# Two-block transformer kernel on one core: first block's output projection in three rounded products, feature by feature, with reordered norm, head-sum and feed-forward steps

## What is computed

```python
def readout(o_sum, g, u):
    o = rmsnorm(o_sum, onorm_g).reshape(Bn, Ln, HG_WIDTH).astype(g.dtype) * jax.nn.silu(g)
    return jnp.concatenate([multiscale_pool(u, pool_w, pool_scale), o], axis=-1) @ w_out
...
x = x + g1 * rmsnorm(y_lat, norm_g[l, 1])
f_lat = swiglu(rmsnorm(x, norm_g[l, 2]) * (1.0 + sc2) + sh2, ffn_w_in[l], ffn_w_out[l])
```

## Time and profile before

| what | value |
|---|---|
| time of the runs, us | 2217.25, 2224.48, 2217.38 (median 2217.38) |
| profiled execution's own time, us | 2223.95 |
| its span in the trace, us | 2222.0 |
| mean granted clock of PE | 0.986 of full |
| bytes read from memory | 370.84 MB |

### The profile page before, as it was taken

One profiled execution on the slowest core, in us unless ns is written; L12 is line 12 of the kernel. 1 busy time (PEld: TensorE's weight loads), 2 busy tenths in 40 slices (PEclk: granted clock), 3 DMA queues, 4 the chain that ended last, 5 costly groups with the idle time before them and its releaser, 6 DMA issues. The chain is left out here.

```text
span 2222.0 us, 32315 instructions
## 1 busy us (share of the span) xinstructions
PE 2151.3 (97%) x13514; PEld 1851.3 (83%) x13514; DVE 1401.9 (63%) x1602; ACT 986.8 (44%) x1114; POOL 173.4 (8%) x94
## 2 busy tenths in 40 slices
PE   6999999999999999999999999999999999999999
PEld 4887788888888857888888898888988897878888
DVE  4367845666766456656665678656665687566665
ACT  3312333444544234444444555445444565254444
POOL 0065600000000000000100011000100012001000
PEclk8999999999999999999999999999999998999999
DMA  8227913455455412355555533555455442124552
GB/s 334 106 100 295 412 74 131 165 191 192 160 189 189 169 72 76 138 192 189 200 189 189 189 133 142 189 189 189 167 191 190 170 166 100 36 91 163 191 192 79
DMA packets 52609, 373.28 MB, mean 168 GB/s; under 512 B 5792, under 2 KB 6816, under 8 KB 7968
## 3 DMA queue, kind: packets, MB, share of 16 engines
q1 hardware_dynamic: 51632, 367.71, 44.9%
q0 software_dynamic: 880, 4.19, 0.5%
HBM read 370.84 MB, written 1.05 MB: 167 GB/s over the span
## 5 line engine op out<-in xcount | busy, mean ns | idle before, releaser
L500 DVE TENSOR_TENSOR ring_r<-ring,AR_r 128x2048 fp32r<-128x2048 f32 x286 | 655.3, 2298 | 267.3 <-ACT AR_r L494 267.1
L494 ACT ACTIVATE AR_r<-ring 128x2048 fp32r<-128x2048 f32 x286 | 545.0, 1911 | 326.2 <-PE PS L397 195.0
L376 PE MATMUL PS<-AR_r 128*128 128x512 f32 x2240 | 533.2, 390 | 0.0
L376 PEld LDWEIGHTS PS<-AR_r 128*128 128x128 f32 x2240 | 415.6, 188 | 83.1
L380 PEld LDWEIGHTS PS<-AR_r,ring_r 128*128 128x128 f32 x2240 | 287.2, 191 | 10.9
L380 PE MATMUL PS<-AR_r,ring_r 128*128 128x256 f32 x2240 | 290.6, 283 | 0.0
L541 ACT ACTIVATE AR<-PS 128x512 f32<-128x512 f32 x140 | 83.7, 598 | 418.6 <-PE PS L380 418.6
L395 PE MATMUL PS<-AR_r 128*128 128x512 f32 x616 | 241.4, 392 | 0.0
L396 PE MATMUL PS<-ring_r,AR_r 128*128 128x512 f32 x616 | 241.1, 391 | 0.0
L397 PE MATMUL PS<-AR_r 128*128 128x512 f32 x616 | 240.4, 390 | 0.0
L397 PEld LDWEIGHTS PS<-AR_r 128*128 128x128 f32 x616 | 116.0, 188 | 24.7
(11 more groups left out here) (394 smaller groups left out, 2927.2 us busy)
## 6 DMA issues: line engine op xcount, KB each, us to landing
ring<-stream SPq DMA_DIRECT2D x346, 1024.0 KB, 4.8
X<-xt SPq DMA_DIRECT2D x1, 2048.0 KB, 9.0
AR<-bias POOLq DMA_DIRECT2D x1, 1536.0 KB, 6.5
AR<-pt POOLq DMA_DIRECT2D x2, 512.0 KB, 4.5
out<-X SPq DMA_DIRECT2D x4, 256.0 KB, 2.1
AR<-invc SPq DMA_DIRECT2D x1, 512.0 KB, 15.3
X<-negl POOLq DMA_DIRECT2D x1, 512.0 KB, 6.3
H<-wax POOLq DMA_DIRECT2D x1, 512.0 KB, 7.2
```

The source lines that it names most:

```text
L376: pe.matmul(PS[:, (6, 4)[half] + j, :], block(w_hi_of(tag, i + half), j, k), X_PARTS[:, k, :], start=(k == 0), stop=False, skip_group_chec ...
L494: act.activation(w_hi_of(tag, i), ring[:, n % SLOTS, :], ACT.Identity).then_inc(split_hi, 1)
L500: dve.tensor_tensor(RING_R[:, n % SLOTS, :], ring[:, n % SLOTS, :], w_hi_of(tag, i), ALU.subtract).then_inc(split_lo, 1)
```

## The change

1. `mix0_out` becomes a split product, by chunks of 256 input features (the host lays the weights out that way): for each chunk 24 products of 128 x 512 (2 token tiles, 2 halves of the output, 2 feature tiles, 3 terms), four chunks of lat, then chunk 0 of ctx, the turn, chunks 1 and 2 of ctx, the norm's sums, chunk 3 of ctx.
2. ACT and DVE get the four weight splits, and the rounding and the rest of the eight input tiles.
3. Order of the norm's steps: all multiplications before the scalings; the additions to X before the splits; in two places the first half of the tokens is scaled before the last statistics.
4. `pe_turn_tokens` after the attention layer, and `pe_turn_both`, wait for each half of the tokens by itself.
5. The low-weights phase at the entry of a feed-forward goes chunk by chunk.
6. `mix3`: half of chunk 13 between the two groups of head sums, the other half between the spreads; the sums wait for the logarithms only; the split of chunk 15 comes before the head norms on ACT and DVE.

```diff
-SPLIT_OUTS = ('mix1_out', 'mix2_out', 'mix3_out')
+SPLIT_OUTS = ('mix0_out', 'mix1_out', 'mix2_out', 'mix3_out')
...
             for i in chunks:
                 pe.wait_ge(split_lo, SPLIT_BASE[tag] + i + 1)
-            for k in range(DT):
-                products(k, True, X_HI)
+                for k in range(DT):
+                    products(k, True, X_HI, of=(i,))
...
+            for q in range(GROUPS):
+                dve.tensor_tensor(SQ[:, pair(q), cols], src[:, pair(q)], r, ALU.mult).then_inc(S["scaled"], S.mark("scaled", (tag, q)))
             for q in range(GROUPS + 1):
                 if q < GROUPS:
-                    dve.tensor_tensor(SQ[:, pair(q), cols], src[:, pair(q)], r, ALU.mult).then_inc(S["scaled"], S.mark("scaled", (tag, q)))
...
+                for k in (*range(4, DT), *range(4)) if apart and t == 0 else range(DT):
+                    if apart and k == 0:
+                        pe.wait_ge(S["normed"], S.at("normed", (tag, t)))
+                    if apart and k == 4:
+                        pe.wait_ge(S["token_high"], S.at("token_high", (tag, t)))
...
+            stats(1, 0)
+            if first_early:
+                scale(0)
+            stats(1, 1)
+            gather(1)
...
+            if nxt:
+                dve_split_chunk(dve, nxt, 1)
+            dve.wait_ge(order.sem, order.n)
             dve.wait_ge(S["residual"], S.at("residual", (tag, GROUPS - 1)))
+            if nxt:
+                dve_split_input(dve, nxt, X[:, :, c])
...
+            def out_chunk(i, key):
+
+                if key == lat:
+                    pe.wait_ge(split_lo, SPLIT_BASE["mix0_out"] + i + 1)
+                    pe.wait_ge(S["mixer_low"], S.at("mixer_low", ("mix0", i)))
+                for t in range(2):
+                    for h in range(2):
+                        first = T + t * P if key == lat else t * P
+                        if i == 0 and key == lat:
+                            pe.wait_ge(S["mixer_output"], S.at("mixer_output", ("mix0 taken", 2 * t + h)))
+                        for f in range(2):
+                            k, ws = 2 * i + f, slice(f * D + h * 512, f * D + (h + 1) * 512)
+                            w_hi, w_lo = w_hi_of("mix0_out", i)[:, ws], RING_R[:, (START["mix0_out"] + i) % SLOTS, ws]
+                            for n, (x, w) in enumerate(((CAT0_HI(k), w_hi), (CAT0_HI(k), w_lo), (CAT0_LO[:, k, :], w_hi))):
+                                ins = pe.matmul(PS[:, (LOW if key == lat else HIGH)[2 * t + h], :], x[:, first:first + P], w, start=(i + f + n == 0),
+                                                stop=(i == 3 and f == 1 and n == 2), skip_group_check=True)
...
+            for i in range(4):
+                out_chunk(i, lat)
+            pe.wait_ge(S["o_rinv"], S.at("o_rinv", HEADS - 1))
+            out_chunk(0, ctx)
             pe_turn_tokens(pe, lat, TOK1[0], LOW)
-            pe_tokens(pe, "mix0_out", ctx, CAT0, 0, 0, 1, 5, False)
+            out_chunk(1, ctx)
+            out_chunk(2, ctx)
             pe_norm(pe, ("ffn0_pre", 0), LAT, 0)
-            for h in range(2):
-                pe_tokens(pe, "mix0_out", ctx, CAT0, 0, 1, h, 6 + h, True)
+            out_chunk(3, ctx)
...
+            for i in range(2):
+                dve_split_chunk(dve, "mix0_out", i)
+            dve.wait_ge(S["mixed"], S.at("mixed", HEADS - 1))
+            for q in range(2):
+                dve.wait_ge(S["x_hi"], S.at("x_hi", ("mix0_out", q)))
+                dve.tensor_tensor(CAT0_LO[:, pair(q), :], CAT0[:, pair(q), :], POOL_HI[:, pair(q), :], ALU.subtract).then_inc(
+                    S["mixer_low"], S.mark("mixer_low", ("mix0", q)))
...
             z_chunk(12)
             head_sums((4, 5, 6, 7))
+            z_half(13, 0)
             head_sums((0, 1, 2, 3))
-            for h in range(4):
+            for h in range(2):
                 spread(h)
+            z_half(13, 1)
             for h in range(0, 2):
                 head_products(h)
-            z_chunk(13)
+                spread(h + 2)
...
-            for i in range(2):
-                dve_split_chunk(dve, "ffn2", i)
-            dve_rms_tokens(dve, order, "ffn1_lat", 0, LOW, TOK1[0], need_tokens(dve, "ffn1_lat", "ffn1_lat", FFN_LAST))
+            dve_split_chunk(dve, "ffn2", 0)
+            dve_rms_tokens(dve, order, "ffn1_lat", 0, LOW, TOK1[0], need_tokens(dve, "ffn1_lat", "ffn1_lat", FFN_LAST), first_early=True)
...
-    parts["mix0_out"] = chunks_in(g["ab_w_out"][0])
+    parts["mix0_out"] = chunks_out(g["ab_w_out"][0])
```

More of the change, by code:

```diff
@@ L293, in pe_chunks_as_features_come, with products @@
             tiles = [(i, j, bank) for i, bank in zip(chunks, banks) for j in range(2)]
-            def products(k, low_weights, x, first=False, last=False):
-                for i, j, bank in tiles:
+            def products(k, low_weights, x, first=False, last=False, of=tuple(chunks)):
+                for i, j, bank in (tile for tile in tiles if tile[0] in of):
                     w = slice(k * 256 + j * P, k * 256 + (j + 1) * P)
@@ L704, in dve_add_turned @@
+            if first_early:
+                scale(0)
+            stats(1, 1)
+            gather(1)
+            if not first_early:
+                scale(0)
+            scale(1)
         def dve_add_turned(dve, order, tag, banks, g, s, nxt=None):
             c = STREAM[s]
[L707 to L719, removed]
+            for q in range(GROUPS):
+                dve.wait_ge(S["turned_back"], S.at("turned_back", (tag, q)))
+                for k in (2 * q, 2 * q + 1):
+                    ins = dve.scalar_tensor_tensor(out=X[:, k, c], in0=PS[:, banks[q], (k % 2) * T:(k % 2 + 1) * T], scalar=mod_of(g, k, s),
+                                                   in1=X[:, k, c], op0=ALU.mult, op1=ALU.add)
+                    if k % 2 == 0:
+                        ins.then_inc(order.sem, order.step())
+                ins.then_inc(S["residual"], S.mark("residual", (tag, q)))
@@ L884, in pe_mix0 @@
-            pe_tokens(pe, "mix0_out", ctx, CAT0, 0, 0, 0, 4, False)
+            def out_chunk(i, key):
[13 more added lines that the diff above has]
+                                                stop=(i == 3 and f == 1 and n == 2), skip_group_check=True)
+                        if i == 3 and (key == lat or (t, h) != (1, 1)):
+                            ins.then_inc(S["tokens_done"], S.mark("tokens_done", (key, t, h)))
+                if key == ctx:
+                    ins.then_inc(multiplied, 1)
@@ L955, in act_mix0 @@
                 act.activation(SQ[:, 4 + h, :], SQ[:, 4 + h, :], ACT.Exp, scale=-0.5).then_inc(S["o_rinv"], S.mark("o_rinv", h))
+            act_split_chunk(act, "mix0_out", 2, free=START["mix0_out"])
+            for h in range(HEADS):
+                act.wait_ge(S["mixer_output"], S.at("mixer_output", (0, h)))
+                act.activation(SQ_R[:, h, :], GS[:, h, :], ACT.Identity).then_inc(S["x_hi"], S.mark("x_hi", ("mix0_out", 2 + h)))
+            act_split_chunk(act, "mix0_out", 3, free=START["mix0_out"])
         def dve_mix0(dve, order):
@@ L1250, in pe_mix1 @@
                 ins.then_inc(multiplied, 1)
-            pe_turn_tokens(pe, "mix1_post", TOK1[0], HIGH)
+            pe_turn_tokens(pe, "mix1_post", TOK1[0], HIGH, apart=True)
             pe_norm(pe, "ffn1_pre", LAT, 0)
@@ L2031, in spread @@
                 if h < 4:
[L2032 removed]
+                    pe.wait_ge(S["head_rinv"], S.at("head_rinv", ("log", h)))
                 else:
```

93 lines of the change are left out of this document (57 added, 36 removed).

## The result

| | runs | median, us | lowest to highest |
|---|---|---|---|
| before | 4 | 2219.95 | 2217.25 to 2224.48 |
| changed | 4 | 2203.82 | 2202.34 to 2205.73 |

The ratio is 0.9926, with an interval of 0.991 to 0.9941: 16.1 us less where 18.9 were forecast. The time of 2203.82 us lies inside the stated range, 5.3 us above the forecast of 2198.5; 2.6 us of that is because the kernel before, with a fourth run, has a median of 2219.95 instead of 2217.38. The profiled execution of the changed kernel took 2202.34 us, its span is 2200.5 us and its granted clock 0.990.

A forecast was written before the change was run, and what follows sets the result against it. PE, busy 97% of the span, was taken to bound the kernel. Terms -6.4 - 3.8 - 1.2 - 7.5 = -18.9 us, off the median of 2217.38, gave 2198.5 us; range 2189 to 2208.

The forecast's parts named there:

- Part 4: `mix3`: half chunks remove the wait between head sums and bring head 4's products sooner; -7.5 us, between -4 and -9.
- A: Rival: `mix0`'s gain is lost in DVE's list, the wait before the feed-forward growing to 12 us; 2205 us, chance 0.13.
- Rival B: `mix3` is bound by DVE and ACT, so half chunks only move PE's wait; 4 us there, 2202 us, chance 0.15.
- Rival D: POOL is held up fully by DVE through the shared port, `ffn1_lat` to `ffn2` gains zero; 2199.7 us, chance 0.06.
- Part 1: `mix0` output products: PE work -12.1 us, partly taken back by a new wait and the clock; -6.4 us, between -4.5 and -8.5.
- The clock: Entry of `ffn0_lat`: the new wait, longer than 4.49 us, lowers PE's rate behind it; 2.1 us added.
- Part 2: Behind the attention layer: transposes by halves lie in PE's wait, ACT's roundings run back to back; -3.8 us, between -2 and -5.
- Part 3: `ffn1_lat` to `ffn2`: statistics and additions to X go ahead of splits; -1.2 us, between -2 and +1.
- The -2.0 us: `ffn1_lat` to `ffn2`: turn's second half about 1.1 us sooner, first phase finished another 0.9 us sooner.
- POOL's share: `ffn1_lat` to `ffn2`: later X_LO and DVE splits beside POOL's residual scalings take back 0.8 us.
- C: Rival: second phases stay where they were, only the products and little else pay; -9 us, 2208.4 us, chance 0.09.
- E: Rival: the 192 `mix0` output products run at 1.2 GHz, so slower; +40.1 us, 2238.6 us, chance 0.03.

The follow-up runs named there:

- only_output: Only the `mix0` output products changed; norms, turns, entries and `mix3` as in the kernel before: 2214.15 us, 0.9967 of the kernel before.
- entry_reordered: Changed kernel, with the first ctx half's statistics taken amid the modulation at `ffn0_lat`'s entry and that half scaled before the modulation's scalings: 2195.64 us, 0.9895 of the kernel before.
- mix3_ahead: Changed kernel with `mix3`'s chunk 14 taken ahead, in pieces before the products of heads 2, 3 and 4: 2201.8 us, 0.991 of the kernel before.
- again: The changed kernel unchanged, measured a second time against the kernel before: 2207.14 us beside 2221.69 us, ratio 0.9930.
- entry_and_ahead: Changed kernel with both the reordered entry to `ffn0_lat` and chunk 14 of `mix3` taken ahead in pieces: 2192.93 us, 0.9878 of the kernel before.
- xlo_first: Changed kernel with DVE's split of `ffn2`'s chunk 1 put behind the splits of the activations: 2205.32 us, 0.9938 of the kernel before.

## Why the prediction was right, point by point

**Sum and sign.** The change is faster by 16.1 us (15.5 in the second comparison) where 18.9 were forecast; on the profiled execution's own time it had 2205 and the changed kernel's took 2202.34. The sum by the timeline, -21.5 us, is larger, since it sets an execution of the kernel before that was near its slowest against the fastest of the changed kernel. Set against the same old code in other runs where there are any, the parts are some 7.0, 3.4, 0.7 and 4.1 us, 15.2 in all, which agrees with the times. The forecast counted its parts on the one slow execution and took them off the median; that put some 1.8 us too much into part 4. The time alone does not tell the forecast from rivals A, B and D (2205, 2202 and 2199.7 us); the traces do.

**Part 1, forecast -6.4.** Trace -9.09 + 1.55 = -7.5; alone, `only_output`, -7.3 by the time and -6.2 by the trace. PE's work fell as counted (0.227 us for each of 192 products, 0.228 forecast). The new wait was forecast as 6.3 us and is 6.25, with DVE's late statistics as its cause, which `entry_reordered` shows: with them moved, the wait is 0.56 us. The clock was put at +2.1 us and took 1.55, and 1.4 to 2.4 over the runs. The wait comes out right only with the reordered norm steps: with the old order it is 7.7 us, 1.5 us more, where the forecast had put their share at 0.3.

**Part 2, forecast -3.8.** Trace -2.08 - 2.47 = -4.55, and -3.4 against the same old code in other runs. The forecast took the 3.32 us of the transposes for the price of the 2.84 us wait, but in `only_output` they take 1.94 us behind that same wait. From L408 of `ffn0_lat` to the entry the change gives 1.0 us against that run, where 1.8 were counted, and behind the entry 2.5, where 2.0 were counted: that the two misses cancel is luck. ACT's roundings took 4.04 us where 4.4 were counted.

**Part 3, forecast -1.2.** Trace -0.33, and the term that was mis-sized is POOL's. The -2.0 us came (-1.9). POOL's share was put at +0.8 and PE's waits for it were 1.45 us. Four scalings took 9.63 us, where four at 1.47 us alone would take 5.9: 3.75 us were lost, nearly all of the 3.9 us in which DVE's splits ran beside them (1075.86 to 1079.78 us). The rule of the Trainium skill ("SBUF — State Buffer", section "SBUF: two separate sides") that a whole instruction is held up fits that; the part that it would bring near zero came out at -0.33 in this pair of traces and at -0.7 against the old norm steps in the other runs, so between the rule and my -1.2. Rival D was right on POOL and not quite on the part.

**Part 4, forecast -7.5.** Trace -4.9 to head 4, -4.1 by the last row of the experiments' table, and 3.8 by undoing it: the largest miss. The failed step is "I take off 1.5 us for low-rate stretches behind the new short waits". The waits themselves were forecast at 0.7 and 1.0 us and are 0.55 and 0.72. But the clock fell behind the first of them: head 3's products and spread took 4.0 us instead of 2.04, and chunk 14 took 7.96 instead of 5.8. That is 4.1 us instead of 1.5, the whole miss in this pair of traces. In the executions where the clock fell later it is 3.2 us, so 1.7 too much; there the rest of the miss is the 1.8 us by which the kernel before, in the trace that the count started from, was slower than the same code in other runs. `mix3_ahead`, where those waits are filled, has the clock at 1.00 and gives 4.4 to 5.4 us back. DVE's wait that it removes is 5.28 us in the changed kernel and 4.34 in `again`; less the clock's 4.1 and 3.2 that leaves 1.2 us each time, which I take to be the earlier place of head 4's products. No run separates the two. Rival B has the size, 4 us, for another reason, DVE and ACT being full; DVE waited 5.28 us, so it was not that.

**The rivals.** A fell: the wait was 6.25 us and not 12. C fell: 16 us, not 9, and each part shows in the traces, the third with 0.3 to 0.7 us. E fell: the 192 products ran at the 2.4 GHz level throughout.

## What to carry over

Count a short wait between short products on PE not by its length but by what runs behind it: here 0.55 + 0.72 us of waiting cost 4.1 us of rate, and 0.55 + 1.01 cost 3.2, and the remedy was to put products that are ready anyway into the waits. The length alone does not tell the price: in `entry_and_ahead` waits of 1.16 and 2.88 us at the end of the heads left the clock at 1.00. And count a gain from more than one execution of the old code: here 1.8 us of part 4 belonged to one execution and not to the code. Where PE's work shrinks by 12 us, look which list becomes the longest at the next joint; moving one half's statistics forward there was worth as much as the rewriting of the products. Whether an engine bounds a stage is read off its waits and its busy share of a window there: DVE with 14.28 of 20 us and a wait of 5.28 for PE was not the bound at head 4, with 18.99 it was.

## What was not expected of the hardware

- The clock fell behind waits that the rows of before gave no example of: in two traces it fell behind 0.55 us among the heads' products, and PE was then at 1.2 GHz for 10.2 us; in five it held there and fell behind the next wait of 1.01 or 1.02 us, for 6.8 us. 0.56 us before dense products at the entry of `ffn0_lat` cost nothing in three traces.
- What the clock costs behind one and the same wait varies: 5.50, 5.55, 5.62, 5.74, 6.31, 6.38, 6.42 and 6.51 us for the same 32 products behind 6.2 to 7.7 us. The longer waits did not give the larger losses.
- DVE and POOL hold each other up in both directions. With POOL's scalings started earlier, DVE's splits of 0.62 us took 0.78 and those of 2.29 took 2.66, while POOL's fell from 2.41 to 2.09 each. Together they lose 3.75 us in the changed kernel, all of it POOL's, and 3.84 us in `xlo_first`, 2.48 of it POOL's and 1.36 DVE's: the loss changes sides and stays.
